# Feed-forward GEMMs of a transformer block in fp32r: plain three-term products, and one level of Strassen's seven products

## What is computed

```python
        h2 = rms_norm(x, norm2_w[l]) * (1.0 + scale2) + shift2
        g, u = jnp.split(h2 @ w_ffn_in[l], 2, axis=-1)
        x = x + gate2 * ((jax.nn.silu(g) * u) @ w_ffn_out[l])
```

## Time and profile before

| what | value |
|---|---|
| time, median of 3 executions | 2836.54 us (2836.48 to 2837.02) |
| span of the profiled execution | 2835.1 us |
| PE busy | 2729.9 us, 96% of the span |
| DVE busy | 1386.4 us, 49% |
| ACT busy | 773.8 us, 27% |
| POOL busy | 342.4 us, 12% |
| DMA traffic | 380.04 MB, 134 GB/s over the span |

### The profile page before, as it was taken

How to read it: one execution, slowest core, us unless ns; L and a number is a source line. 1 busy time by engine, 2 the same in 40 slices (tenths; PEclk the granted TensorE clock), 3 DMA queues, 4 the chain that set the end, 5 groups by cost and what they waited for, 6 DMA issues and landing times.

```text
span 2835.1 us, 34770 instructions
## 1 busy us (share of the span) xinstructions
PE 2729.9 (96%) x12300; PEld 2250.8 (79%) x12300; DVE 1386.4 (49%) x1969; ACT 773.8 (27%) x1051; POOL 342.4 (12%) x306
## 2 busy tenths in 40 slices
PE   4689999999999999999799999999999999999998
PEld 4568888788888888888588888888888888888887
DVE  7978878743333467755633333242423333332423
ACT  3233333333333322222322222222222222222221
POOL 3642323210000011132300000000000000000000
PEclk8799999999999999999999999999999999999999
DMA  9866666533333377766223233333333332333232
GB/s 317 265 209 197 179 176 175 158 95 96 96 104 93 114 229 234 232 196 215 65 97 96 96 96 96 96 96 96 96 96 96 96 96 96 97 96 97 95 98 86
DMA packets 392089, 380.04 MB, mean 134 GB/s; under 512 B 13061, under 2 KB 379929, under 8 KB 391545
## 3 DMA queue, kind: packets, MB, share of 16 engines
q1 hardware_dynamic: 384056, 354.09, 40.4%
q0 software_dynamic: 5888, 21.37, 2.2%
q10 hardware_dynamic: 2112, 4.19, 0.4%
HBM read 362.83 MB, written 16.78 MB: 134 GB/s over the span
## 4 chain that ended last, share of the span: by engine, by line
PE 91%; DVE 3%; issue 2%; POOL 2%; ACT 1%; DMA 1%; SPq 0%; POOLq 0%; DVEq 0%; ACTq 0%
PE bank L517 28%; PE bank L519 28%; PE bank L518 28%; PE bank L648 1%; DVE ada_acc L1055 1%; PE bank L528 1%; POOL ada_sum L1341 1%; DVE h_t L1273 1%; PE bank L669 1%; PE bank L637 1%; PE bank L624 0%; DMA x_rows<-in_x 0%; PE bank L682 0%; POOL h_lo L1356 0%; POOL w_lo L1368 0%
## 5 line engine op out<-in xcount | busy, mean ns | idle before, releaser
L1030 DVE TENSOR_TENSOR w_lo<-w_raw,w_hi 128x1024 fp32r<-128x1024 f32 (+1 forms) x460 | 569.5, 1239 | 1302.3 <-ACT w_hi L793 1301.8
L517 PE MATMUL bank<-h_hi,w_hi 128*128 128x512 f32 x2704 | 1065.3, 394 | 18.0 <-POOL h_lo L1356 18.0
L519 PE MATMUL bank<-h_hi,w_lo 128*128 128x512 f32 x2704 | 1053.7, 390 | 0.0
L518 PE MATMUL bank<-h_lo,w_hi 128*128 128x512 f32 x2704 | 1053.1, 389 | 0.0
L793 ACT ACTIVATE w_hi<-w_raw 128x1024 fp32r<-128x1024 f32 (+1 forms) x460 | 486.1, 1057 | 1587.6 <-PE bank L519 1495.4
L517 PEld LDWEIGHTS bank<-h_hi,w_hi 128*128 128x128 f32 x2704 | 508.2, 188 | 130.9 <-issue 17.0
L519 PEld LDWEIGHTS bank<-h_hi,w_lo 128*128 128x128 f32 x2704 | 508.0, 188 | 107.3
L518 PEld LDWEIGHTS bank<-h_lo,w_hi 128*128 128x128 f32 x2704 | 508.4, 188 | 105.3 <-issue 1.9
L1055 DVE SCALAR_TENSOR_TENSOR ada_acc<-w_raw,small_all,ada_acc 128x256 f32<-128x256 f32 x560 | 313.7, 620 | 11.4 <-DMA w_raw<-in_w_ada 11.4
L519 PE MATMUL bank<-u_hi,w_lo 128*128 128x512 f32 x704 | 273.9, 389 | 0.0
L517 PE MATMUL bank<-u_hi,w_hi 128*128 128x512 f32 x704 | 273.9, 389 | 0.0
(11 more groups left out here) (181 smaller groups left out, 1768.5 us busy)
## 6 DMA issues: line engine op xcount, KB each, us to landing
w_raw<-in_w_ffn_in SPq DMA_DIRECT2D x176, 512.0 KB
w_raw<-in_w_ada SPq DMA_DIRECT2D x160, 512.0 KB
w_raw<-in_w_ffn_out SPq DMA_DIRECT2D x88, 512.0 KB
w_raw<-in_w_in SPq DMA_DIRECT2D x132, 256.0 KB
w_raw<-in_w_in SPq DMA_DIRECT2D x64, 512.0 KB
shift_raw<-in_w_ada SPq DMA_DIRECT2D x32, 512.0 KB, 8.0
w_raw<-in_w_out SPq DMA_DIRECT2D x32, 512.0 KB
gate_fm<-gst POOLq DMA_DIRECT2D x16, 512.0 KB, 3.2
```

The lines of the kernel that those rows point to most:

```text
L517: nc.tensor.matmul(bank[b][:], lhsT=whi[:, cols], rhs=xh, start=first_k, stop=False)
L518: nc.tensor.matmul(bank[b][:], lhsT=whi[:, cols], rhs=xl, start=False, stop=False)
L519: mm = nc.tensor.matmul(bank[b][:], lhsT=wlo[:, cols], rhs=xh, start=False, stop=last_k)
L1030: v.tensor_tensor(lo, raw, hi.bitcast(F32), ALU.subtract).then_inc(lo_done, 1)
```

## The change

Both FFN GEMMs are done by one level of Strassen's scheme in Winograd's form. A pair of 128-row tiles of the contraction is one half each, a pair of 256-column blocks of the weights the other split, and the 512 tokens are cut into two halves of 256 (HB). Of the 2 x 2 blocks of each operand four are taken and three or four sums are formed, and seven products of blocks replace eight.

- A unit is now 2 row tiles by 512 weight columns (256 of g and 256 of u in part 1), still 512 KB. There are 22 groups (FG) of 8 units in part 1, one for each 256 hidden features, and in part 2 3 chunks of 8, 8 and 6 pairs by 4 output groups: 176 + 88 = 264 units. A unit is 7 products x 2 column tiles x 3 terms = 42 matmuls of 256 moving columns, 11,088 in all. Each product has a PSUM bank of its own.
- DVE forms the weight sums of a unit (`sum_first`, `sum_second`, `sum_third`; 512, 256 and 256 columns) and the low parts of three raw blocks (`low_p`, 768 columns) and of four sums (`low_s`, 1024). ACT makes the high parts (`high_p`, `high_s`). The split weights have three slots.
- After the last unit of a group ACT takes two banks and DVE combines the seven products in seven instructions of 512 columns (`evict`). In part 1 ACT takes silu, DVE multiplies (`u_product`), and POOL forms the Strassen combinations of the u pair and its low part, 1792 columns; ACT makes its high part (`u_high`). The 14 blocks of a pair, 1.8 MB, are stored to DRAM (`u_fm`) and come back before part 2 into `mov`, which held h2's pairs in part 1, in the places that PE has just read for the last time.
- The h2 stage forms h2's combinations and low parts on DVE, pair by pair, in among the weight work of group 0.
- The residual lies in DRAM (`y_fm`), is loaded, added to in 8 instructions of 256 columns for an output group (`accumulate`) and stored again; in the last chunk it is transposed group by group and stored to the output.
- The loop of 11 iterations is gone: all units are written out.

The rows below are what stands in the queues of the engines, before and now. First DVE in the FFN, before: the low parts of a g and a u quarter (`w_lo`), the product with silu (`u_full`), its low part, and the start of the residual additions.

The diff, cut to its core:

```diff
--- before.py
+++ after.py
@@
-E_R, E_N, E_I = D_R + D_N * D_I, 24, DFF // (UK * P)
+E_R = D_R + D_N * D_I
+HB = 2 * P
+BLOCKS = 7
+CW = BLOCKS * HB
+PAIRS = KD // 2
+FG = DFF // HB
+CHUNKS = (8, 8, 6)
+OG = D // (2 * HB)
+def ffn_units():
+
+    table = []
+    for g in range(FG):
+        for s in range(PAIRS):
+            table.append((1, g, s, PAIRS, s, None, g))
+    p0 = 0
+    for c, size in enumerate(CHUNKS):
+        for n in range(OG):
+            for s in range(size):
+                table.append((2, FG + c * OG + n, s, size, p0 + s, c, n))
+        p0 += size
+    return table
...
+        w_sum = [at("w_sum0", WHI + 14 * T, 4 * HB), at("w_sum1", FORGET + 7 * T, 4 * HB)]
+        w_slot = [at("w_slot0", WHI, 2 * CW, F32R), at("w_slot1", WHI + 7 * T, 2 * CW, F32R),
+                  at("w_slot2", FORGET, 2 * CW, F32R)]
...
@@ SyncE: the loads
+            for v, (part, g, s, steps, p, ch, n) in enumerate(UNITS):
+                if v >= RING:
+                    sp.wait_ge(lo_p, v - RING + 1)
+                    sp.wait_ge(sums_done, 3 * (v - RING + 1))
...
@@ TensorE
+            products = ((0, 0, 1), (5, 5, 5), (1, 2, 2), (6, 3, 3), (4, 4, 4), (3, 1, 6), (2, 6, 0))
+                if idx in (0, 4):
+                    pe.wait_ge(ev_act, 2 * (g - 1) + (1 if idx == 0 else 2))
+                else:
+                    pe.wait_ge(ev_dve, 7 * (g - 1) + (0, 1, 2, 3, 0, 6, 7)[idx])
...
+            for v, (part, g, s, steps, p, ch, n) in enumerate(UNITS):
+                if g == 0:
+                    pe.wait_ge(q_ready, s + 1)
+                if part == 2 and n == 0:
+                    pe.wait_ge(mov_landed[s], 16 * (ch + 1))
+                pe.wait_ge(lo_p, v + 1)
+                pe.wait_ge(lo_s, v + 1)
+                for idx, (bk, wb, qb) in enumerate(products):
+                    if s == 0 and g > 0:
+                        bank_free(idx, g)
+                    xh, xl = blk(mov_hi(s), qb), blk(mov_lo(s), qb)
+                    for t in range(2):
+                        cols = slice(wb * HB + t * P, wb * HB + (t + 1) * P)
+                        wh, wl = slot_hi(v)[:, cols], slot_lo(v)[:, cols]
+                        dst = bank[bk][:, t * HB:(t + 1) * HB]
...
@@ ScalarE
+            def high_p(v):
+                act.wait_ge(e_raw[v % RING], raw_landed_at(v))
+                if v >= 3:
+                    act.wait_ge(e_unit, v - 2)
+                elif v:
+                    act.wait_ge(unit_done, E_R)
+                nc.scalar.activation(blk(slot_hi(v), 0, 3), blk(e_raw_slot(v), 1, 3), ACT.Copy).then_inc(hi_p, 1)
+            def high_s(v):
+                act.wait_ge(sums_done, 3 * v + 3)
+                nc.scalar.activation(blk(slot_hi(v), 3, 4), sums(v)[:], ACT.Copy).then_inc(hi_s, 1)
...
+            def evict(g):
+                act.wait_ge(prod_done, 6 * g + 1)
+                if g == 0:
+                    act.wait_ge(q_ready, PAIRS - 1)
+                elif g <= FG:
+                    act.wait_ge(u_ready, g)
...
+            def u_high(g):
+                act.wait_ge(u_comb, 3 * g + 3)
...
+            def load_mov(v):
...
+                act.wait_ge(e_unit, v + 1)
+                act.wait_ge(u_stored, 16 * (p0 + CHUNKS[nxt]))
+                act.dma_start(mov[:, s * 2 * CW:(s + 1) * 2 * CW].bitcast(F32), u_fm[p0 + s]).then_inc(mov_landed[s], 16)
...
+            for w in range(NV):
+                if w + 1 < PAIRS:
+                    h2_high(w + 1)
+                if w + 2 < PAIRS:
+                    h2_block(w + 2)
+                if w + 2 < NV:
+                    high_p(w + 2)
+                    high_s(w + 2)
+                if w >= 1:
+                    load_mov(w - 1)
+                if ends(w) is not None:
+                    evict(ends(w))
...
@@ VectorE
+            def evict(g, w):
...
+                v.tensor_tensor(c12, bank[5][:], c11, ALU.subtract).then_inc(ev_dve, 1)
...
+                dve.wait_ge(e_unit, w + 1)
+                dve.wait_ge(ev_dve, 7 * g + 4)
+                v.tensor_tensor(c12, bank[2][:], c12, ALU.subtract).then_inc(ev_dve, 1)
...
+            for w in range(NV):
+                if w + 1 < PAIRS:
+                    h2_combine(w + 1)
+                if w + 3 < NV:
+                    sum_first(w + 3)
+                if w + 2 < NV:
+                    low_p(w + 2)
+                if w + 3 < NV:
+                    sum_second(w + 3)
+                if w + 2 < NV:
+                    low_s(w + 2)
+                if w + 3 < NV:
+                    sum_third(w + 3)
+                if w + 1 < PAIRS:
+                    h2_low(w + 1)
+                if ends(w) is not None:
+                    evict(ends(w), w)
+                g = ends(w - 1)
+                if g is not None and g < FG:
+                    u_product(g)
+                elif g is not None:
+                    accumulate(g, (4, 5, 0, 1, 2, 3, 6, 7))
...
@@ GpSimd
-            for k in range(KD):
-                low(KD + k, k % 2, k, h2_full)
+            for u in range(FG):
+                pool.wait_ge(u_mul, 2 * u + 2)
+                g.tensor_tensor(blk(b0, 4, 2).rearrange("p (b n) -> p b n", b=2),
+                                blk(b0, 0)[:, None, :].to_broadcast([P, 2, HB]),
+                                blk(b0, 1, 2).rearrange("p (b n) -> p b n", b=2), ALU.subtract).then_inc(u_comb, 1)
+                pool.wait_ge(u_comb, 3 * u + 1)
+                g.tensor_tensor(blk(b0, 6), blk(b0, 1), blk(b0, 5), ALU.subtract).then_inc(u_comb, 1)
+                pool.wait_ge(u_comb, 3 * u + 2)
+                g.tensor_tensor(blk(b0, 7), blk(b0, 3), blk(b0, 6), ALU.subtract).then_inc(u_comb, 1)
+                pool.wait_ge(u_hi_done, u + 1)
+                g.tensor_tensor(u_stage[:, CW:2 * CW], blk(b0, 1, 7), u_stage[:, 0:CW].bitcast(F32), ALU.subtract
+                                ).then_inc(u_ready, 1)
+                pool.wait_ge(u_ready, u + 1)
+                pool.dma_start(u_fm[u], u_stage[:].bitcast(F32)).then_inc(u_stored, 16)
```

421 lines of the change are left out of this document (284 added, 137 removed).

## The result

The changed kernel takes 2810.62 us (2806.99 to 2811.08, 4 runs) where the kernel before takes 2836.64 on the same chip (2836.48 to 2837.02, 4 runs): a ratio of 0.9906, interval 0.9892 to 0.9920. It is faster by 0.9%, 26 us, where I had forecast 97. The time lies in the stated range of 2700 to 2825 us, toward its slow end. The profiled execution has a span of 2808.9 us.

A forecast was written before the change was run, and what follows sets the result against it. PE's rate was taken to bound the FFN. 1460 to group 0's end, 829.5 for 21 groups, 425 for part 2, 5.2 transposes, 6 refills and 12 tail gave 2737.7, predicted as 2739 us; range 2700 to 2825.

The forecast's parts named there:

- PE's new rate: FFN matmuls of 256 columns: 115 ns each (113 to 0.12 us), so 4.83 us a unit (4.76 to 5.04).
- the second weight load: In the trace before, behind an fp32r matmul of 256 columns, it began 0.12 us after the first: the upper bound.
- Most is absorbed; I take 2 us each, 6 in all: Refills of `mov` at three group ends: 6.6 us against 4.83 a unit, mostly absorbed, 6 us in all (0 to 39).
- Rival 2: Refills of `mov` starve the weights, long rows being favoured by the queues: 33 us more, 2772 us; chance 8%.
- The tie of PE and DVE: Part 1 groups: 38.6 us for PE and 38.6 for DVE with POOL's turns, taken as 39.5 (38.1 to 42.6).
- rival 1: Part 1: DVE binds because its instructions don't overlap, 42.6 us a group, 65 us more, 2804 us; chance 21%.
- The sign that I had named for rival 1: PE waiting at units after `w_slot` low parts throughout part 1 would show that rival 1 holds.
- POOL's turns: Part 1: POOL and DVE take turns, so POOL's time is DVE's time, 6.7 us a group.
- rival 3: Part 1: POOL doesn't get its turn, delaying ACT's bank 0 and PE; groups of 48 us, 2917 us; chance 13%.
- The start of the FFN: After the h2 stage's first work, PE starts the FFN at 1374.3 us, not 1367.7.
- the tail: The end after the last matmuls: additions, transposes, copies and stores of the last output group, 12 us.
- PE idle half the time to 1460: Group 0: PE waits for the h2 stage's 11.2 us a unit, idle half the time until about 1460 us.

The follow-up runs named there:

- the halved one: The kernel before, with each FFN matmul of 512 moving columns issued as two of 256, same arithmetic: 2955.99 us, ratio 1.0414.
- the bare stream: A kernel of its own without the block, only streams of 240 matmuls each on resident data: fp32r with 256 columns started every 120 ns.
- uhigh: The changed kernel with ACT taking the high part of a u pair one unit later, POOL keeping its work: 2797.25 us, ratio 0.9848.

## Why the prediction was wrong

**PE's new rate: the term that was mis-sized.** I took 115 ns from half of 226.5 and 0.12 from the second weight load. The upper bound, 120, was right. Halving 226.5 took for granted that the 13.3 ns over 512/2.4 shrink with the columns; they don't. 256 units of 5.04 us instead of 4.83 are 54 us; since I had given part 1 groups 39.5, above that pitch, 36 of them count against the sum. The changed kernel, the halved one and the bare stream all show 120. The second load of the earlier trace rows was the better witness: it had a short matmul ahead of it, the halved stream had none. My own bound of 5.04 us a unit was the result.

**"Most is absorbed; I take 2 us each, 6 in all": the term that was wrong by its reasoning.** The refills cost 32 us, 3 ahead of unit 176 and 29.1 after. The step that failed is that a pair due a group later, and a raw ring of four units, absorb it. A pair has that slack and doesn't use it: it lands 24 to 39 us early. The weights, due within some four units, have little and get late behind it, up to 25.6 us to land, and DVE waits 46.5 us for them. Behind each long wait comes the lower clock, 7.6 of the 32 us, which the term had no place for. Rival 2, given 8%, had this mechanism, the refills starve the weights, and about the size: 6.6 us for each of 22 units is 34 us over a pitch of 5.04. Its reason, the long rows, is borne out as far as the weights go: with rows of 2 KB they land in 7.2 us and DVE's wait is gone. That this would give the time back isn't shown, since ACT's issues took it. The rule of the Trainium skill (DMA: Bandwidth & Descriptors, "Queues, rings and completion order") that queues take turns by packets fits these shares. That 34 meets 32 is in part luck: the sum has no lower clock in it, and about nine units wait, not 22.

**The tie of PE and DVE: right for DVE, and the wrong reason for what showed.** DVE's unit is 3.28 us in the trace (L1415 at 1685.02 and again at 1688.30) where 3.3 was forecast, with the overlap; rival 1 fell. At 120 ns the tie is gone, 38.6 against 40.3. Still a group took 41.0, since DVE's slack was spent on waiting for ACT. The sign that I had named for rival 1, waits at units after low parts of `w_slot` throughout part 1, did appear (in 19 of the groups), so it was no sign of rival 1: `uhigh` removes it and leaves DVE's work as it is.

**POOL's turns.** That POOL and DVE take turns was right, and DVE beside the 1792 columns lasted over 4 us. "In turns" was wrong for POOL: while DVE has work it gets none. That is rival 3's mechanism, at a far smaller price: one of the four instructions waits, 6.9 us (8.22 less 1.29), and then DVE runs out of free slots and POOL is let in for the rest. The chain it lengthens ends in ACT's `u_high`, and by the code's order in 0.7 us a group, 15 in all; not in bank 0, which I had named.

**Right as they stood.** The start of the FFN (1373.75 for 1374.3), group 0 with 11.09 us a pair for 11.2, the weight load hidden in a pitch of 120, the transposes (4.4 us for 5.2), the tail (12.15 for 12). "PE idle half the time to 1460" was a third (busy 53.78 of 81.10 us), with the lower clock making up the rest. ACT's share stays small (37%), but its order costs time in part 1 and in group 0. The direction was right; the gain, 26 us of 97, is the sum of the terms above. That the time still lies in 2700 to 2825 is luck: the upper end was set for rival 1, which did not happen.

## What to carry to other kernels

Before a scheme with fewer but shorter matmuls, price the short ones by a fixed part and a part per column, not by halving: here an eighth of the products was saved, 12.5% of PE's time in the FFN, and the fixed 13.3 ns took back 5 of the 12.5. Where a whole operand is exchanged while another streams in, ask at what rate both are requested and which of them has slack: a transfer that is asked for early takes its share from one that is due soon. Add what the engine loses in clock after each wait. And a cure has its own price: seven short transfers for a long one held up the engine that issued them. And an instruction given to an idle POOL that shares data access with a busy DVE is late by as long as DVE stays busy: nothing urgent may stand in order behind what waits for it.

## What the runs showed of the hardware

- An fp32r matmul with 128 weight columns starts every columns/2.4 + 13.3 ns (512, 384, 320 and 256 columns), and every 111.7 ns with 192 or 128. With 64 weight columns 256 moving columns pass in 113.3 ns and 128 in 60.0, but 512 take 229.9. bf16 with 128 weight columns: 2.5 ns over the columns.
- Behind a wait of 5.3 us PE was granted 0.50 (1.2 GHz) and its matmuls started 213 ns apart instead of 120 for about 5 us.
- POOL's tensor_tensor next to a dense DVE waits until DVE has a hole (8.22 us for 1.29, median of 22; it ends 1.15 us after DVE's stop), and a DVE instruction that comes while POOL runs waits for its end (4.21 for 0.95).
- A looped body on PE of twice the instructions lost about 2.5 us at its start, ten times; the cause was not isolated.
- Short rows bring the other queue's transfers a larger share (7.2 us to land instead of 12.4) at the same total rate (388 and 396 GB/s). Issuing seven transfers for one into full queues held ACT up to 8.8 us at a time.
